# The last pair's round of a stick-breaking attention kernel: VectorE in another order, and eight lower parts of the output weights on GpSimd

## The chip, the cores and the metric

The kernel runs on one core of a Trainium2 chip. What counts is the device time of one execution in microseconds. Five engines run side by side, each through its own list of instructions, and meet at semaphores: TensorE (PE) multiplies, VectorE (DVE) and ScalarE (ACT) work element by element and may read the accumulators (PSUM), GpSimd (POOL) works on the on-chip memory SBUF alone, and SyncE (SP) issues the transfers. Transfers are carried by 16 DMA engines.

## The reference

With one layer only the stick-breaking attention is computed: norm, one input projection to q, k, v and gate, 16 heads of 64, a gated output projection, a residual and a final norm.

```python
h = rmsnorm(x, norm_g[0])                       # x: 1 x 1024 x 1024, float32
q, k, v, gate = jnp.split(h @ w_in, 4, axis=-1)
z = jnp.einsum('bhqd,bhkd->bhqk', q, k) * scale
log_beta = jax.nn.log_sigmoid(z)
log_1m = jnp.where(mask, log_beta - z, 0.0)     # mask: key before query
after = lax.cumsum(log_1m, axis=3, reverse=True) - log_1m
a = jnp.where(mask, jnp.exp(log_beta + after), 0.0)
o = jnp.einsum('bhqk,bhkd->bhqd', a, v)
y = (o * jax.nn.silu(gate)) @ w_out
out = rmsnorm(x + y, final_g)
```

## The kernel before

Products that need float32 are made of three (or two) matmuls of rounded numbers: each operand is split into a high part, a rounded copy, and a **lower part**, the rest after subtraction. A lower part is one `tensor_tensor` with `subtract`, and the high part comes before it, mostly from ScalarE.

The heads are worked on in eight pairs. A round of a pair has 16 **slots**; slot s makes the scores of one head (s // 8) and one block of 128 queries (s % 8), so that the width grows from 128 to 1024 keys in slots 0 to 7 and again in 8 to 15. In every slot the chain is: TensorE makes z (L581); ScalarE makes two sigmoids of it, `rest` (L809) and beta in `a_group` (L811); VectorE turns `rest` into a product along the keys by a scan (L1016); GpSimd multiplies the two (L1115, `a_ready`); TensorE transposes the blocks of the result into `t_ps` (L644); ScalarE copies them to `aT` or `aT_pad` (L794) and VectorE makes the lower part (L1000, `t_lo`); TensorE multiplies with v into `o_ps` (L632). Transposes of a slot take a group of four query blocks that was finished four slots before: those of slot 8 need `a_ready` of slot 7. When a group is done, ScalarE shifts (L786) and VectorE adds (L990) it into `oT`; in slots 1 and 5 GpSimd multiplies `oT` by the gate (L1103), and in slots 2 and 6 ScalarE and VectorE split it (L800, L1006) for SyncE to store.

Between these steps TensorE has other work that fills it up. In the last pair's round it is the gate's projection in slots 0 to 7 (L486) and, from slot 8 on, early blocks of the output projection (L561), listed by slot in `EARLY_BY_SLOT`: two in each of slots 8, 9 and 10, one in slot 11. In a slot they come before the products with v. An early block b of the first output tile needs the stored output of pair b back in `hT` (`o_loaded`, L427) and the output weight block b in its two parts (`wo_ready` at least b + 1).

A gate half is evacuated in slots 0, 4 and 8: ScalarE copies it to `stage` and takes its sigmoid, and VectorE multiplies the two (L982, `gate_ready`).

The **output weight blocks** 0 to 7 come in the last pair's round too. `wo_raw` is a ring of four; SyncE loads blocks 0 to 3 early, and block n from 4 on when `wo_ready` has reached n - 3 (L420). ScalarE makes the high part of the blocks listed for the slot in `WO_BY_SLOT` (`wo_hi`), and VectorE, behind its scan of the same slot, the lower part (`wo_lo_part`, L314, `wo_ready`):

```python
WO_BY_SLOT = {5: (0,), 6: (1,), 7: (2,), 8: (3,), 9: (4, 5), 10: (6,), 12: (7,)}
```

The loads of SyncE stand in one written order: load 4, outputs of pair 2, load 5, output 3, two stores (L395), load 6, outputs 4 and 5, load 7, output 6, two blocks of x, and then the other halves of the outputs. Each output is two loads, of its high and its lower part.

The order on each engine is that of the program: the functions `slot(p, par, s)` of the engines, called by `over_pairs`. `is_last(p)` is true in the round of the last pair, number 7.

Of the kernel before, what the change touches and what calls it, by code (L numbers as in the profile page):

```python
# [29 lines left out]
HALF = 512  # L30
# [96 lines left out]
def evac_at(p, s):  # L127

    if s % 2 or is_tail(p) or (is_first(p) and s == 0):
        return None  # L130
    number = 2 * UNITS0 + 8 * p + s // 2 - 1
    if s == 0:
        return "g", 1, number
    if is_last(p):
        return ("g", s // 4 - 1, 2 * UNITS0 + 8 * p + s // 4 - 1) if s in (4, 8) else None
    return kind_of(p, s - 1), ((s - 1) % 4) // 2, number


def gate_at(p, s):

    evac = evac_at(p, s)
    if not evac or evac[0] != "g":
        return None
    return evac[1], 2 * p - 1 if s == 0 else 2 * p + evac[1]
# [33 lines left out]
def stick_breaking_layer(nc, x, norm_g, w_in, w_out, final_g, out):  # L178
# [3 lines left out]
    with ExitStack() as ctx:  # L182
# [666 lines left out]
        def _(dve):  # L849
# [80 lines left out]
            def heads_lo(kind, par, half, buf, count):  # L930

                dve.wait_ge(qk_hi, count)
                cols = slice(half * HALF, (half + 1) * HALF)
                for hh in range(2):
                    rows = slice(HD * hh, HD * hh + HD)
                    other = slice(HD - HD * hh, 2 * HD - HD * hh)
                    to = q_of(par, hh) if kind == "q" else k_of(par, hh, False)
                    last = nc.vector.tensor_tensor(to[other, cols], stage[rows, buf, :],  # L938
                                                   to[rows, cols].bitcast(F32), ALU.subtract)
                last.then_inc(qk_split, 1)  # L940
# [27 lines left out]
                wait_wo(dve, n)  # L968
                nc.vector.tensor_copy(w_out_of(n // KB, 0)[:, n % KB, :], wo_raw[:, n % WO_RING, :]).then_inc(wo_hi, 1)

            def slot(p, par, s):
                evac = evac_at(p, s)
                if evac:
                    kind, half, h = evac
                    if kind in "kq":
                        heads_lo(kind, 1 - par, half, half, 4 * p + 5 + half + (2 if kind == "q" else 0))
                if gate_at(p, s):

                    half, number = gate_at(p, s)
                    dve.wait_ge(gate_sig, number + 1)  # L980
                    cols = slice(half * HALF, (half + 1) * HALF)
                    nc.vector.tensor_tensor(gate[:, cols], stage[:, half, :], gate[:, cols], ALU.mult  # L982
                                            ).then_inc(gate_ready, 1)
                if s % 4 == 1 and av_at(p, s - 1) and (not is_tail(p) or s < 9):
                    _, _, ohh, grp, _ = av_at(p, s - 1)[-1]
                    group = {1: -1, 5: 0, 9: 1, 13: 2}[s]
                    dve.wait_ge(o_shift, 4 * p + group)
                    rows = slice(HD * ohh, HD * ohh + HD)
                    cols = slice(grp * HALF, (grp + 1) * HALF)
                    nc.vector.tensor_tensor(oT[rows, cols], o_ps[rows, :], oT[rows, cols], ALU.add  # L990
                                            ).then_inc(o_summed, 1)

                for t, av, _, grp, j in (units_at(p, s - 1) if s else av_at(p, 0)):
                    rel = max(0, j - GQ * grp)
                    dve.wait_ge(t_hi, t_base(p) + t + 1)
                    if rel == GQ - 1:
                        hi, lo = aT_pad[:, 0, P:2 * P], aT_pad[:, 1, P:2 * P]
                    else:
                        hi, lo = aT[:, av % 2, 0, rel * P:HALF], aT[:, av % 2, 1, rel * P:HALF]
                    nc.vector.tensor_tensor(lo, t_ps[t % 2][:, rel * P:HALF], hi.bitcast(F32), ALU.subtract  # L1000
                                            ).then_inc(t_lo, 1)
                if s in (2, 6) and not is_first(p):
                    half = s // 4
                    dve.wait_ge(o_hi, 2 * p - 1 + half)
                    hi, lo = split_of(p, half)
                    nc.vector.tensor_tensor(lo, oT[:, half * HALF:(half + 1) * HALF], hi.bitcast(F32),  # L1006
                                            ALU.subtract).then_inc(o_lo, 1)
                if is_tail(p):
                    return

                width = P * (s % 8 + 1)
                span = rest[:, s % 2, S - 1:(S - 1 - width if width < S else None):-1]
                if is_first(p) and s == 0:
                    dve.wait_ge(restart_ready, 1)
                dve.wait_ge(rest_ready, SLOTS * p + s + 1)
                nc.vector.tensor_tensor_scan(span, span, restart[:, S - 1:(S - 1 - width if width < S else None):-1],  # L1016
                                             0.0, ALU.mult, ALU.max).then_inc(scan_done, 1)
                if v_t_at(p, s) is not None:
                    t = v_t_at(p, s)
                    v_lo(1 - par, s // 8, t_base(p) + t, t % 2)  # L1020
                if is_last(p):
                    for n in WO_BY_SLOT.get(s, ()):
                        dve.wait_ge(wo_hi, n + 1)
                        wo_lo_part(nc.vector, n)
                if is_last(p) and s in PARTIAL_SLOTS:

                    n = PARTIAL_SLOTS.index(s)
                    dve.wait_ge(partial_done, n + 1)
                    dve.wait_ge(xs_loaded[n], 16)
                    nc.vector.tensor_tensor(stage[:, n, :], proj_ps[:, :], stage[:, n, :], ALU.add  # L1030
                                            ).then_inc(partial_sum, 1)
# [44 lines left out]
        @block.gpsimd  # L1076
        def _(pool):
            pool.dma_start(g_col[:, :], norm_g).then_inc(g_loaded, 16)

            nc.gpsimd.memset(ident[:, :], 0.0).then_inc(zeros_ready, 1)  # L1080
            pool.wait_ge(zeros_ready, 1)
            nc.gpsimd.affine_select(out=ident[:, :], in_=ident[:, :], compare_op=ALU.not_equal, fill=1.0, base=0,
                                    pattern=[[-1, P]], channel_multiplier=1).then_inc(consts_ready, 1)
            nc.gpsimd.memset(restart[:, 0:S - P], 0)
            pool.wait_ge(consts_ready, 2)
            nc.gpsimd.tensor_copy(restart[:, S - P:S], ident[:, :]).then_inc(restart_ready, 1)

            def lo_w(n, ring, part):
                pool.wait_ge(w_hi, n + 1)
                to = w_split[:, ring, :, 4 * part:4 * part + 4, :]  # L1090
                nc.gpsimd.tensor_tensor(to[:, 1], w_raw[:, part, :].rearrange("p (b n) -> p b n", b=4),  # L1091
                                        to[:, 0].bitcast(F32), ALU.subtract).then_inc(w_ready, 1)

            for n in range(2 * UNITS0 + 2):
                lo_w(n, (n // 2) % 2, n % 2)

            def slot(p, par, s):
                if s in (1, 5) and not is_first(p):
                    half = s // 4
                    pool.wait_ge(o_summed, 4 * p - 1 + half)  # L1100
                    pool.wait_ge(gate_ready, 2 * p - 1 + half)
                    cols = slice(half * HALF, (half + 1) * HALF)
                    nc.gpsimd.tensor_tensor(oT[:, cols], oT[:, cols], gate[:, cols], ALU.mult  # L1103
                                            ).then_inc(o_gated, 1)
                if is_tail(p):
                    return

                i = s % 8
                width = P * (i + 1)
                a = a_g[i // GQ][:, i % GQ, 0:width]  # L1110
                if is_first(p) and s == 0:
                    pool.wait_ge(consts_ready, 2)
                pool.wait_ge(beta_ready, SLOTS * p + s + 1)
                pool.wait_ge(scan_done, SLOTS * p + s + 1)
                nc.gpsimd.tensor_tensor(a, a, rest[:, s % 2, S + 1 - width:S + 1], ALU.mult  # L1115
                                        ).then_inc(a_ready, 1)
                if s % 2 and not is_last(p):
                    part = s % 4 // 2
                    lo_w(2 * (UNITS0 + 4 * p + s // 4 + 1) + part, (UNITS0 + 1 + s // 4) % 2, part)

            over_pairs(pool, slot)


            for n in range(KB, 2 * KB):
                pool.wait_ge(wo_hi, n + 1)
                wo_lo_part(nc.gpsimd, n)
# [24 lines left out]
```

## Time and profile before

| | us |
|---|---|
| median of 3 runs | 697.34 |
| lowest and highest of them | 697.03, 698.51 |
| the profiled execution, its own time | 696.88 |
| its span, first to last instruction | 694.8 |
| busy in the span: TensorE | 670.2 (96%) |
| VectorE | 481.4 (69%) |
| ScalarE | 426.4 (61%) |
| GpSimd | 282.0 (41%) |

The profile gives every instruction's start and length from the span's start. An instruction's length begins when its waits on semaphores are over, so that what it waits for behind that, a port for instance, is in its length. The last pair's round runs from about 546 to 610 us, its slots 5 to 10 from about 564 to 590. "Idle before" is the time for which the engine had nothing running, with the engine, tile and line that ended it. TensorE's weight loads run beside its matmuls.

### The profile page before, as it was taken

The numbers are of one execution on the slowest core, as the hardware profiler recorded it, in microseconds if no ns is written. First come the engines' busy times: TensorE is split into PE (matmuls) and PEld (weight loads), VectorE is DVE, ScalarE is ACT, GpSimd is POOL, SyncE is SP. The second block draws the span as 40 slices with busy tenths as digits, with TensorE's granted clock in tenths as the row PEclk, the third lists the DMA queues.
The fourth block names the chain that finished last, engine by engine and source line by source line (L and its number), as shares of the span: only waits on it lengthen the run. The fifth ranks groups of instructions, "written<-read, shape, count | busy, mean of one in ns | idle before, by whom it ended". The sixth has DMA issues, their size and how long they took to land.

```text
span 694.8 us, 10872 instructions
## 1 busy us (share of the span) xinstructions
PE 670.2 (96%) x3426; PEld 563.4 (81%) x3426; DVE 481.4 (69%) x636; ACT 426.4 (61%) x795; POOL 282.0 (41%) x225
## 2 busy tenths in 40 slices
PE   5999999999999999999999999999999997999995
PEld 4787888888888888888888888888888776888884
DVE  5835666776678677867776677667766798735565
ACT  5614767676767676767676767666766675622333
POOL 2122434453545445444554454435353543315100
PEclk9999999999999999999999999999999999999999
DMA  7131301241114110410042014201420148523332
GB/s 288 46 95 43 92 31 31 61 122 33 31 51 131 31 33 33 136 44 20 25 129 67 16 32 121 76 15 30 121 60 30 61 137 290 211 92 94 125 145 92
DMA packets 28122, 57.64 MB, mean 83 GB/s; under 512 B 3376, under 2 KB 3376, under 8 KB 28080
## 3 DMA queue, kind: packets, MB, share of 16 engines
q1 hardware_dynamic: 25312, 51.13, 24.0%
q10 hardware_dynamic: 2736, 6.03, 2.3%
q8 instruction: 16, 0.26, 0.2%
q14 instruction: 26, 0.21, 0.1%
q0 software_dynamic: 32, 0.00, 0.0%
HBM read 37.23 MB, written 11.53 MB: 70 GB/s over the span
## 4 chain that ended last, share of the span: by engine, by line
PE 90%; DVE 5%; ACT 2%; DMA 1%; POOL 1%; issue 1%; ACTq 0%; DVEq 0%; POOLq 0%
PE proj_ps L486 46%; PE o_ps L632 10%; PE z_ps L581 9%; PE t_ps L644 9%; PE z_ps L561 8%; PE proj_ps L561 4%; PE o_ps L486 2%; DVE rest L1016 2%; PE t_ps L495 1%; DMA a_group<-x 1%; DVE gate L982 1%; ACT stage L719 1%; PE z_ps L506 1%; DVE arena L314 0%; DVE aT L1000 0%
## 5 line engine op out<-in xcount | busy, mean ns | idle before, releaser
L486 PE MATMUL proj_ps<-hT,w_split 128*128 128x512 f32 x1464 | 359.9, 394 | 2.2 <-DVE hT L889 1.4
L486 PEld LDWEIGHTS proj_ps<-hT,w_split 128*128 128x128 f32 x1464 | 270.0, 188 | 57.6 <-DVE hT L889 2.3
L1115 POOL TENSOR_TENSOR a_group<-a_group,rest 128x128 f32<-128x128 f32 (+7 forms) x128 | 158.0, 1235 | 300.0 <-DVE rest L1016 300.0
L1016 DVE TENSOR_TENSOR_SCAN rest<-rest,restart 128x128 f32<-128x128 f32 (+7 forms) x128 | 203.6, 1591 | 16.0 <-ACT rest L809 15.5
L1000 DVE TENSOR_TENSOR aT<-t_ps,aT 128x512 fp32r<-128x512 f32 (+2 forms) x160 | 93.1, 607 | 35.1 <-ACT aT L794 33.6
L794 ACT ACTIVATE aT<-t_ps 128x512 fp32r<-128x512 f32 (+2 forms) x160 | 80.2, 532 | 59.2 <-PE t_ps L644 57.6
L1091 POOL TENSOR_TENSOR w_split<-w_raw,w_split 128x512 fp32r<-128x512 f32 x64 | 91.7, 1434 | 38.1 <-DVE w_split L851 38.1
L581 PE MATMUL z_ps<-arena 128*128 128x512 f32 (+2 forms) x384 | 96.3, 366 | 0.3 <-DVE arena L938 0.3
L938 DVE TENSOR_TENSOR arena<-stage,arena 64x512 fp32r<-64x512 f32 x64 | 44.0, 687 | 67.9 <-ACT arena L739 67.3
L809 ACT ACTIVATE rest<-z_ps 128x128 f32<-128x128 f32 (+7 forms) x128 | 83.9, 655 | 8.9 <-PE z_ps L581 8.6
L644 PE MATMUL t_ps<-ident,a_group 128*128 128x128 f32 x576 | 84.6, 274 | 0.4 <-POOL a_group L1115 0.4
L811 ACT ACTIVATE a_group<-z_ps 128x128 f32<-128x128 f32 (+7 forms) x128 | 84.4, 659 | 0.0
L632 PE MATMUL o_ps<-aT,arena 128*128 128x512 f32 (+2 forms) x320 | 82.7, 364 | 1.7 <-DVE aT L1000 1.7
L644 PEld LDWEIGHTS t_ps<-ident,a_group 128*128 128x128 f32 x576 | 70.0, 142 | 8.5 <-issue 0.6
L719 ACT ACTIVATE stage<-proj_ps 128x512 f32<-128x512 f32 x61 | 36.5, 598 | 61.3 <-PE proj_ps L486 61.3
L632 PEld LDWEIGHTS o_ps<-aT,arena 128*128 128x128 f32 x320 | 59.5, 188 | 16.6 <-DVE aT L1000 4.2
L581 PEld LDWEIGHTS z_ps<-arena 128*128 128x128 f32 x384 | 59.6, 190 | 5.2 <-DVE arena L938 0.8
L561 PE MATMUL z_ps<-arena,hT 128*128 128x512 f32 x246 | 57.7, 391 | 0.0
L786 ACT ACTIVATE oT<-o_ps 64x512 f32<-64x512 f32 x32 | 19.0, 593 | 62.2 <-PE o_ps L632 62.2
L561 PEld LDWEIGHTS z_ps<-arena,hT 128*128 128x128 f32 x246 | 45.8, 188 | 9.4
L990 DVE TENSOR_TENSOR oT<-o_ps,oT 64x512 f32<-64x512 f32 x32 | 22.0, 689 | 25.6 <-ACT oT L786 25.3
L746 ACT ACTIVATE w_split<-w_raw 128x512 fp32r<-128x512 f32 x56 | 35.9, 641 | 0.6
(86 smaller groups left out, 460.7 us busy)
## 6 DMA issues: line engine op xcount, KB each, us to landing
w_raw<-w_in SPq DMA_DIRECT2D x64, 256.0 KB, 2.6
arena<-arena SPq DMA_DIRECT2D x32, 256.0 KB, 4.3
wo_raw<-w_out SPq DMA_DIRECT2D x16, 256.0 KB, 3.8
o_hi_scratch<-o_split SPq DMA_DIRECT2D x14, 256.0 KB, 2.1
o_lo_scratch<-o_split SPq DMA_DIRECT2D x14, 256.0 KB, 2.4
hT<-o_hi_scratch SPq DMA_DIRECT2D x14, 256.0 KB, 4.9
hT<-o_lo_scratch SPq DMA_DIRECT2D x14, 256.0 KB, 6.0
a_group<-x SPq DMA_DIRECT2D x14, 256.0 KB, 3.6
```

The lines of the kernel that those rows point to most:

```text
L486: mm = nc.tensor.matmul(bank[:, :], w_split[:, ring, wl, b, :], hT[:, hl, b, half * HALF:(half + 1) * HALF], start=(b == 0 and n == 0), st ...
L561: mm = nc.tensor.matmul(bank[:, :], hT[:, ol, b, tokens], w_out_of(nh, wl)[:, b, :], start=(b == first and m == 0), stop=(b == last and m ...
L581: mm = nc.tensor.matmul(z[:, c0:c1], q, k_of(par, hh, swapped)[:, c0 - first:c1 - first], start=not swapped, stop=swapped)
L632: mm = nc.tensor.matmul(o_ps[:, c:HALF], v_of(apar)[:, j, 2 * ahh:2 * ahh + 2, :] .rearrange("p x d -> p (x d)"), moving, start=(j == 0 an ...
L644: last = nc.tensor.transpose(t_ps[t % 2][:, i2 * P:(i2 + 1) * P], a_g[grp][:, i2, j * P:(j + 1) * P], ident[:, :])
L794: nc.scalar.activation(to, t_ps[t % 2][:, rel * P:HALF], ACT.Copy).then_inc(t_hi, 1)
L809: nc.scalar.activation(rest[:, s % 2, S - width:S], z_ps[s % 2][:, first:first + width], ACT.Sigmoid, scale=-SCALE).then_inc(rest_ready, 1)
L811: nc.scalar.activation(a_g[grp][:, i % GQ, 0:width], z_ps[s % 2][:, first:first + width], ACT.Sigmoid, scale=SCALE).then_inc(beta_ready, 1)
L1000: nc.vector.tensor_tensor(lo, t_ps[t % 2][:, rel * P:HALF], hi.bitcast(F32), ALU.subtract).then_inc(t_lo, 1)
L1016: nc.vector.tensor_tensor_scan(span, span, restart[:, S - 1:(S - 1 - width if width < S else None):-1], 0.0, ALU.mult, ALU.max).then_inc(s ...
L1091: nc.gpsimd.tensor_tensor(to[:, 1], w_raw[:, part, :].rearrange("p (b n) -> p b n", b=4), to[:, 0].bitcast(F32), ALU.subtract).then_inc(w_ ...
L1115: nc.gpsimd.tensor_tensor(a, a, rest[:, s % 2, S + 1 - width:S + 1], ALU.mult).then_inc(a_ready, 1)
```

## The change

In the last pair's round VectorE does the sum of a finished group and the lower parts of `aT` (now the function `heads_out`) before the gate product; in the other rounds the order is as it was. And in that round the lower parts of blocks 0 to 7 of the output weights are made by GpSimd, in the same slots, each behind GpSimd's own product of the slot.

```diff
-            def slot(p, par, s):
-                evac = evac_at(p, s)
...
+            def heads_out(p, s):
+
                 if s % 4 == 1 and av_at(p, s - 1) and (not is_tail(p) or s < 9):
...
+            def slot(p, par, s):
+                if is_last(p):
+                    heads_out(p, s)
+                evac = evac_at(p, s)
...
+                if not is_last(p):
+                    heads_out(p, s)
                 if s in (2, 6) and not is_first(p):
...
-                if is_last(p):
-                    for n in WO_BY_SLOT.get(s, ()):
-                        dve.wait_ge(wo_hi, n + 1)
-                        wo_lo_part(nc.vector, n)
                 if is_last(p) and s in PARTIAL_SLOTS:
...
                 nc.gpsimd.tensor_tensor(a, a, rest[:, s % 2, S + 1 - width:S + 1], ALU.mult
                                         ).then_inc(a_ready, 1)
+                if is_last(p):
+                    for n in WO_BY_SLOT.get(s, ()):
+                        pool.wait_ge(wo_hi, n + 1)
+                        wo_lo_part(nc.gpsimd, n)
                 if s % 2 and not is_last(p):
```

VectorE, slots 5 to 8 of the last pair's round, before. A row is the line, the operation, what is written and read, and the shape; the scan is called SCALAR_TENSOR_TENSOR here:

```order
L1016 SCALAR_TENSOR_TENSOR rest<-rest,restart 128x768
L314 TENSOR_TENSOR arena<-wo_raw,arena 128x512
L1000 TENSOR_TENSOR aT<-t_ps,aT 128x384
L1006 TENSOR_TENSOR o_split<-oT,o_split 128x512
L1016 SCALAR_TENSOR_TENSOR rest<-rest,restart 128x896
L314 TENSOR_TENSOR arena<-wo_raw,arena 128x512
L1000 TENSOR_TENSOR aT<-t_ps,aT 128x256
L1016 SCALAR_TENSOR_TENSOR rest<-rest,restart 128x1024
L314 TENSOR_TENSOR arena<-wo_raw,arena 128x512
L982 TENSOR_TENSOR gate<-stage,gate 128x512
L1000 TENSOR_TENSOR aT_pad<-t_ps,aT_pad 128x128
L1016 SCALAR_TENSOR_TENSOR rest<-rest,restart 128x128
```

The same place in the changed kernel, whose lines have other numbers (the scan is L1023, the lower parts of aT L989, the gate product L1005, the split L1013):

```order
L1023 SCALAR_TENSOR_TENSOR rest<-rest,restart 128x768
L989 TENSOR_TENSOR aT<-t_ps,aT 128x384
L1013 TENSOR_TENSOR o_split<-oT,o_split 128x512
L1023 SCALAR_TENSOR_TENSOR rest<-rest,restart 128x896
L989 TENSOR_TENSOR aT<-t_ps,aT 128x256
L1023 SCALAR_TENSOR_TENSOR rest<-rest,restart 128x1024
L989 TENSOR_TENSOR aT_pad<-t_ps,aT_pad 128x128
L1005 TENSOR_TENSOR gate<-stage,gate 128x512
L1023 SCALAR_TENSOR_TENSOR rest<-rest,restart 128x128
```

The three L314 are gone from VectorE, and the gate product stands behind the lower part of the padded tile.

GpSimd, slots 5 to 9 of the same round, before:

```order
L1103 TENSOR_TENSOR oT<-oT,gate 128x512
L1115 TENSOR_TENSOR a_group<-a_group,rest 128x768
L1115 TENSOR_TENSOR a_group<-a_group,rest 128x896
L1115 TENSOR_TENSOR a_group<-a_group,rest 128x1024
L1115 TENSOR_TENSOR a_group<-a_group,rest 128x128
L1115 TENSOR_TENSOR a_group<-a_group,rest 128x256
```

and in the changed kernel, where the product of a slot is L1118 and the gating product L1106:

```order
L1106 TENSOR_TENSOR oT<-oT,gate 128x512
L1118 TENSOR_TENSOR a_group<-a_group,rest 128x768
L314 TENSOR_TENSOR arena<-wo_raw,arena 128x512
L1118 TENSOR_TENSOR a_group<-a_group,rest 128x896
L314 TENSOR_TENSOR arena<-wo_raw,arena 128x512
L1118 TENSOR_TENSOR a_group<-a_group,rest 128x1024
L314 TENSOR_TENSOR arena<-wo_raw,arena 128x512
L1118 TENSOR_TENSOR a_group<-a_group,rest 128x128
L314 TENSOR_TENSOR arena<-wo_raw,arena 128x512
L1118 TENSOR_TENSOR a_group<-a_group,rest 128x256
L314 TENSOR_TENSOR arena<-wo_raw,arena 128x512 x2
```

The parts of blocks 0 to 5 now stand between GpSimd's products. TensorE's, ScalarE's and SyncE's orders are the same in both kernels.

## Rows read from the trace of the kernel before

**Rows 1.** Timeline of TensorE, 545 to 611 us: start, length, operation [idle before]

```profile
549.45 0.50 PE L632 MATMUL o_ps<-aT_pad,arena 128*128 128x256 f32 x2 [1.15 <-DVE aT_pad L1000]
...
552.11 1.33 PE L632 MATMUL o_ps<-aT,arena 128*128 128x512 f32 x4
...
573.68 0.51 PE L632 MATMUL o_ps<-aT,arena 128*128 128x256 f32 x2 [1.18 <-DVE aT L1000]
...
574.61 1.55 PE L561 MATMUL proj_ps<-arena,hT 128*128 128x512 f32 x6
580.32 0.79 PE L632 MATMUL o_ps<-aT_pad,arena 128*128 128x256 f32 x2 [4.16 <-DVE aT_pad L1000]
580.91 1.91 PE L644 MATMUL t_ps<-ident,a_group 128*128 128x128 f32 x8
...
586.44 1.54 PE L561 MATMUL proj_ps<-arena,hT 128*128 128x512 f32 x6
...
592.95 3.02 PE L561 MATMUL proj_ps<-arena,hT 128*128 128x512 f32 x12 [0.18 <-DVE stage L1030]
...
610.60 1.06 PE L644 MATMUL t_ps<-ident,a_group 128*128 128x128 f32 x8 [0.39 <-POOL a_group L1115]
```

**Rows 2.** Busy times in windows: five engines, then the clock's share, DMA's, GB/s

```profile
579.00:580.00 1.00, 0.00 (x0) 0.00 (x0) 1.00 (x2) 0.00 (x0) 0.52 (x1) 0.92 0.93 287
...
583.00:584.00 1.00, 1.00 (x5) 0.81 (x4) 0.84 (x2) 1.00 (x4) 0.00 (x0) 0.87 1.09 350
```

**Rows 3.** Timeline of VectorE, 545 to 606 us

```profile
547.24 1.95 DVE L982 TENSOR_TENSOR gate<-stage,gate 128x512 f32<-128x512 f32 x1 [0.75 <-ACT gate L776]
...
549.32 1.29 DVE L1016 TENSOR_TENSOR_SCAN rest<-rest,restart 128x128 f32<-128x128 f32 x1
...
560.97 1.17 DVE L982 TENSOR_TENSOR gate<-stage,gate 128x512 f32<-128x512 f32 x1 [0.62 <-ACT gate L776]
...
565.44 1.75 DVE L1016 TENSOR_TENSOR_SCAN rest<-rest,restart 128x768 f32<-128x768 f32 x1
567.10 1.72 DVE L314 TENSOR_TENSOR arena<-wo_raw,arena 128x512 fp32r<-128x512 f32 x1
...
570.70 2.01 DVE L1016 TENSOR_TENSOR_SCAN rest<-rest,restart 128x896 f32<-128x896 f32 x1
572.64 0.66 DVE L314 TENSOR_TENSOR arena<-wo_raw,arena 128x512 fp32r<-128x512 f32 x1
...
573.55 3.53 DVE L1016 TENSOR_TENSOR_SCAN rest<-rest,restart 128x1024 f32<-128x1024 f32 x1
577.00 0.66 DVE L314 TENSOR_TENSOR arena<-wo_raw,arena 128x512 fp32r<-128x512 f32 x1
577.59 2.48 DVE L982 TENSOR_TENSOR gate<-stage,gate 128x512 f32<-128x512 f32 x1
```

**Rows 4.** Timeline of GpSimd, 545 to 606 us

```profile
565.49 2.79 POOL L1103 TENSOR_TENSOR oT<-oT,gate 128x512 f32<-128x512 f32 x1
568.24 1.99 POOL L1115 TENSOR_TENSOR a_group<-a_group,rest 128x768 f32<-128x768 f32 x1
572.86 2.08 POOL L1115 TENSOR_TENSOR a_group<-a_group,rest 128x896 f32<-128x896 f32 x1 [2.63 <-DVE rest L1016]
577.23 2.29 POOL L1115 TENSOR_TENSOR a_group<-a_group,rest 128x1024 f32<-128x1024 f32 x1 [2.29 <-DVE rest L1016]
```

**Rows 5.** Instructions on wo_raw: ns min/median/max, first and last start

```profile
L314 POOL TENSOR_TENSOR arena<-wo_raw,arena x8: 1294/1298/1490, 632.3 to 643.9; 128x512 fp32r<-128x512 f32 x8
```

**Rows 6.** Timeline of SyncE's issues, 540 to 640 us

```profile
577.69 0.34 SPq L420 DMA_DIRECT2D wo_raw<-w_out  x1
...
579.50 0.43 SPq L427 DMA_DIRECT2D hT<-o_lo_scratch  x1
```

**Rows 7.** us from issue to landing: the issue of 579.50, then the page's median

```profile
hT<-o_lo_scratch SPq DMA_DIRECT2D x1, 256.0 KB, 5.2
...
hT<-o_lo_scratch SPq DMA_DIRECT2D x14, 256.0 KB, 6.0
```

More of the change, by code:

```diff
@@ L969, in wo_hi_part @@
                 nc.vector.tensor_copy(w_out_of(n // KB, 0)[:, n % KB, :], wo_raw[:, n % WO_RING, :]).then_inc(wo_hi, 1)
-            def slot(p, par, s):
-                evac = evac_at(p, s)
[L973 to L983, printed above, removed]
+            def heads_out(p, s):
                 if s % 4 == 1 and av_at(p, s - 1) and (not is_tail(p) or s < 9):
@@ L1001, in slot @@
                                             ).then_inc(t_lo, 1)
+            def slot(p, par, s):
+                if is_last(p):
+                    heads_out(p, s)
+                evac = evac_at(p, s)
+                if evac:
+                    kind, half, h = evac
+                    if kind in "kq":
+                        heads_lo(kind, 1 - par, half, half, 4 * p + 5 + half + (2 if kind == "q" else 0))
+                if gate_at(p, s):
+                    half, number = gate_at(p, s)
+                    dve.wait_ge(gate_sig, number + 1)
+                    cols = slice(half * HALF, (half + 1) * HALF)
+                    nc.vector.tensor_tensor(gate[:, cols], stage[:, half, :], gate[:, cols], ALU.mult
+                                            ).then_inc(gate_ready, 1)
+                if not is_last(p):
+                    heads_out(p, s)
                 if s in (2, 6) and not is_first(p):
```

## The prediction

> **What bounds the kernel now.** I read the chain of waits first, then the timelines of the four engines over the last pair's round, and last SyncE's queue. TensorE is busy nearly everywhere, so a change in this round is worth what it does to TensorE's gaps there, and to waits that are hidden today. The largest gaps are 1.15 us in slot 0, 1.18 us in slot 7, and 4.16 us in slot 8, which ends at 580.32 [rows 1]. The last one costs more than its length: 3.7 us after TensorE stopped (576.16) the granted clock fell from its 2.4 GHz level to the 1.2 GHz one, from 579.84 to 583.26, as the shares 0.92 and 0.87 of two windows give [rows 2]. In it eight transposes took 1.91 us, and 1.06 elsewhere [rows 1].
>
> The gap of slot 8 ends with VectorE's lower part of the padded tile. Ahead of it VectorE ran without a pause: scans, lower parts of aT, three lower parts of output weight blocks (L314) and the gate product [rows 3]. Several took far longer than their work. The gate product took 2.48 us and ended 0.55 us after GpSimd's product of 577.23 (2.29 us, to 579.52); the scan of 1024 took 3.53 us and ended 2.14 us after GpSimd's product of 572.86 (to 574.94); the first L314 took 1.72 us and the second 0.66 [rows 3, 4]. The other way round, GpSimd's gating product dispatched at 565.49 took 2.79 us, and ended 1.09 us after VectorE's scan of 565.44 (to 567.19) [rows 3, 4]. So instructions of VectorE with two SBUF inputs and GpSimd's products take turns, the one dispatched first going first. I call that the port. This is what the sum is made with.
>
> **Part 1, the other order.** It acts in slots 0, 4 and 8. In slot 0 the gate product (547.24, 1.95 us) holds up the lower part, and TensorE loses 1.15 us [rows 1, 3]. With the order changed this gap goes, but the gate product still ends behind GpSimd at 549.19, the next scan still ends at 550.61 behind GpSimd's weight part, and o_sum and two lower parts follow as now, for which TensorE's o_ps of 552.11 waits at the end of slot 1 [rows 1, 3]. Gained: 0 to 0.1 us; I take 0. In slot 4 the gate product (1.17 us from 560.97) stands before lower parts that TensorE hardly waits for, and the scan behind both moves by under 0.1 us: 0. In slot 8 it takes the lower part out from behind 2.48 us. That gain depends on part 2.
>
> **Part 2, the eight lower parts on GpSimd.** Each leaves VectorE (0.66 us free of a wait, [rows 3]) and costs 1.30 us on GpSimd [rows 5], 1.10 when it has waited for the port (the 1.09 above, same shape). Each still needs the port, twice as long as before. In slots 5 to 8 the port has no room. I walk it from 567.19, where the scan of slot 5 ends in both kernels:
> gating product to 568.28 as now; product of slot 5 to 569.8 (1.4 us behind the port now, about 1.5 here; now 570.23 as L314 is ahead); o_split's lower part, 0.55, to 570.35; block 0's part, queued on GpSimd since 569.8 and so ahead of the scan, 1.1, to 571.45; scan of 896, 1.86 behind the port (2.01 free), to 573.3, now 572.71; product of slot 6, 0.15 to start and 1.8, to 575.25; scan of 1024, 2.14, to 577.4, now 577.08; block 1's part 1.1, to 578.5; gate product 0.55, to 579.05; product of slot 7, 1.86 (what 577.23 took once the port was free at 577.66), to 580.9, now 579.52; scan of 128, 0.3, to 581.2; block 2's part to 582.3; product of slot 8, 0.4, to 582.7; block 3's part, 1.3, to 584.0 [rows 3, 4, 5]. ScalarE's copies of the blocks, for which the parts wait too, were there for VectorE's parts of 572.64 and 577.00 [rows 3] and don't hold them.
>
> What TensorE sees of it. The lower part of slot 8 is ready at 577.7 instead of just before 580.32. But three other things come late. First, the second early block of slot 8 needs wo_ready 2, that is block 1's part, at 578.5; today it is hidden. TensorE does it then and goes on with o_ps to about 579.7. Second, the transposes of slot 8 need a_ready of slot 7 at 580.9; they start at 580.91 now [rows 1]. So of the 4.16 us nothing comes back there. Third, in slot 9 the early blocks 2 and 3 need the parts that end at 582.3 and 584.0: blocks done by 584.7, o_ps then, about 0.3 us later than now. The 0.85 us of slow transposes are saved and waited away again here.
>
> **Part 3, SyncE's queue, which is the term that decides.** A raw block is reloaded when a part has been made: load 6 waits for wo_ready 3. Now that is VectorE's L314 of 577.00, done at 577.66, and the load goes out at 577.69; behind it stand the four loads of stored outputs 4 and 5, the last at 579.50 [rows 3, 6]. With block 2's part at 582.3 load 6 goes at 582.33 and the last of the four 1.81 us later, at 584.15. It lands 5.2 us after issue now [rows 7]: 589.35. TensorE wants it in slot 10, in the second of the two early blocks that start at 586.44 and end at 587.98 now [rows 1]. It is hidden by over 3 us today; then it is not: 589.35 and three matmuls of 0.23 give 590.05, 2.07 us later. Output 6, behind load 7, goes at about 585.4, lands by 591 and is wanted at 592.0, and the parts 4 to 6 are done by 586.4, 587.6 and 591.2, each before its use: hidden, by 0.8 us at the least.
>
> After slot 10 VectorE has pauses, and TensorE's gaps are 0.18 us at 592.95 and 0.39 at 610.60 [rows 1]; both end chains that TensorE's own work starts, so they move along. Blocks 6 and 7 on GpSimd free 1.3 us of VectorE where nobody waits for it: 0. The sum is +2.05 us, from 0 (part 1), 0 (slot 8), and +2.05 (slot 10, which contains the +0.3 of slot 9). On the profiled execution's own 696.88 that is 698.9; on the median of 697.34 it is 699.4.
>
> The Trainium skill (Perfetto Trace Analysis, Optimizing Scalar/DVE Operations) says of moving work between VectorE and GpSimd that, since they share a port, it "might not help". By that the sum would be 0; this trace agrees that they take turns (the 2.48 us product, [rows 3]).
>
> **Rivals.** (a) *The gain arrives*: GpSimd's extra parts hide beside VectorE's scans, without turns. Then, from 567.19, the scan of 1024 ends about 576.0, the product of slot 7 about 578.0, transposes 2.9 us earlier; but block 2's part ends about 579.3, 1.6 us after 577.66, so the load lands about 586.3 and slot 10's blocks end about 587.0: 1.0 us gained, 696.3. It needs the port to be free for these parts, against all four stretched rows; were the loads of no account it would be up to 3 us. 0.15. (b) *The loads are hidden after all*, because they land faster from a queue that stood empty: then part 5 of GpSimd, done at 587.6, decides, +0.3, 697.6; between this and the forecast lies up to +1.3. 0.20. (c) *Worse*: the page's median from issue to landing is 6.0 us and not 5.2 [rows 7], +0.8; and TensorE's pieces of idling (3.1, 1.2, 0.8, 0.8 us) bring the clock down again, about +0.9 as the slow transposes show: +3.8, 701.1. For the clock speaks the fall at 579.84, against it that no single gap reaches the 3.7 us before that fall. 0.10. (d) That the change doesn't do what it says: the rows of the order show both parts of it, so this gets no chance of its own. The forecast keeps 0.55, between +1.4 and +3.2.
>
> **The numbers.** 0.2% is 1.4 us, about what a measurement of this kernel can tell from no change. Slower by more: forecast and (c), 0.65. Within: (b) and half of (a), 0.27. Faster by more: the rest of (a), 0.08. The range leaves out that rest and the upper part of (c): 696.5 to 701.2.
>
> **What would show it.** Lower parts of L314 on GpSimd of 1.3 us or more, block 1's ending near 578.5 and block 2's near 582.3; TensorE's gap before slot 8's padded o_ps short, but transposes of slot 8 still near 581; two waits in slots 8 and 9 at L561 for GpSimd's L314, and one in slot 10 for a landing of stored output; slot 10's early blocks ending near 590. Load 6 issued before 580, or transposes of slot 8 before 579.5, would prove the walk wrong; slot 10 without a wait for a landing would leave me with (b).

## The result

The changed kernel takes 700.47 us in the median of 6 runs (699.96 to 701.58); the kernel before took 697.13 beside it (6 runs). The ratio is 1.0044, with a 95% interval of 1.0034 to 1.0054: slower by 3.1 us by the ratio, and by 3.3 us between the two medians. Forecast was +2.05 us, or 699.4 us, in a range from 696.5 to 701.2.

The profiled execution took 701.32 us, its span is 699.5 (before: 696.88 and 694.8). That pair differs by 4.4 us, more than the medians. Of that, 0.81 us come from TensorE's first projection of the last pair's round, which starts at 547.50 and not at 546.69, as it did before. They lie ahead of everything that was changed; that start was anywhere from 546.5 to 547.5 in the profiles of this study. To compare a time of after with one of before, take 0.81 off.

### The profile after

The timeline of TensorE, columns as in rows 1 (start, length, operation, idle before it and what ended it):

```profile
549.59 1.06 PE L644 MATMUL t_ps<-ident,a_group 128*128 128x128 f32 x8 [0.22 <-POOL a_group L1118]
...
552.92 1.33 PE L632 MATMUL o_ps<-aT,arena 128*128 128x512 f32 x4 [0.87 <-DVE aT L989]
...
575.28 0.87 PE L561 MATMUL proj_ps<-arena,hT 128*128 128x512 f32 x3
579.16 1.10 PE L561 MATMUL proj_ps<-arena,hT 128*128 128x512 f32 x3 [3.01 <-POOL arena L314]
...
581.65 1.94 PE L644 MATMUL t_ps<-ident,a_group 128*128 128x128 f32 x8 [0.97 <-POOL a_group L1118]
583.25 2.92 PE L561 MATMUL proj_ps<-arena,hT 128*128 128x512 f32 x6
...
590.50 0.93 PE L561 MATMUL proj_ps<-arena,hT 128*128 128x512 f32 x3 [1.91 <-DMA hT<-o_lo_scratch]
591.81 0.93 PE L561 MATMUL proj_ps<-arena,hT 128*128 128x512 f32 x3 [0.37 <-DMA hT<-o_lo_scratch]
```

These rows answer rows 1. The gap of 1.15 us in slot 0 is gone, and in its place stand 0.22 us for GpSimd's product and 0.87 us one slot later: the o_ps of 552.92 is that of 552.11 before, less 0.81 to the hundredth. In slot 8 the padded product no longer waits 4.16 us for VectorE. The second early block waits 3.01 us for GpSimd's lower part of block 1 instead, and the transposes wait for GpSimd's product. Then in slot 10 both early blocks wait for the landing of a stored output, and the second of them ends at 592.74, which is 591.93 on the clock of before: 3.95 us behind 587.98.

VectorE and GpSimd, slots 6 to 9:

```profile
570.87 3.11 DVE L1023 TENSOR_TENSOR_SCAN rest<-rest,restart 128x896 f32<-128x896 f32 x1
...
574.22 3.82 DVE L1023 TENSOR_TENSOR_SCAN rest<-rest,restart 128x1024 f32<-128x1024 f32 x1
...
578.15 1.50 DVE L1005 TENSOR_TENSOR gate<-stage,gate 128x512 f32<-128x512 f32 x1
579.57 2.21 DVE L1023 TENSOR_TENSOR_SCAN rest<-rest,restart 128x128 f32<-128x128 f32 x1
```

```profile
570.36 1.74 POOL L314 TENSOR_TENSOR arena<-wo_raw,arena 128x512 fp32r<-128x512 f32 x1
574.13 1.77 POOL L1118 TENSOR_TENSOR a_group<-a_group,rest 128x896 f32<-128x896 f32 x1 [2.02 <-DVE rest L1023]
575.86 3.25 POOL L314 TENSOR_TENSOR arena<-wo_raw,arena 128x512 fp32r<-128x512 f32 x1
579.07 2.44 POOL L1118 TENSOR_TENSOR a_group<-a_group,rest 128x1024 f32<-128x1024 f32 x1
581.47 1.39 POOL L314 TENSOR_TENSOR arena<-wo_raw,arena 128x512 fp32r<-128x512 f32 x1
...
583.19 1.28 POOL L314 TENSOR_TENSOR arena<-wo_raw,arena 128x512 fp32r<-128x512 f32 x1
```

Every one of the walk's turns can be read off here. The scan of 896, 2.01 us before [rows 3], is 3.11 long, because block 0's part went first and ended at 572.10. The scan of 1024 waits for the product that ends at 575.90; block 1's part, dispatched at 575.86, waits for the scan (578.04) and ends at 579.11; the gate product follows, to 579.65, the product of slot 7 to 581.51, the scan of 128, and block 2's part to 582.86.

SyncE's issues, and below them the time from issue to landing of the transfer of 584.71:

```profile
579.13 0.33 SPq L420 DMA_DIRECT2D wo_raw<-w_out  x1
...
580.92 0.43 SPq L395 DMA_DIRECT2D o_lo_scratch<-o_split  x1
582.88 0.34 SPq L420 DMA_DIRECT2D wo_raw<-w_out  x1
583.26 0.45 SPq L427 DMA_DIRECT2D hT<-o_hi_scratch  x1
583.76 0.43 SPq L427 DMA_DIRECT2D hT<-o_lo_scratch  x1
584.23 0.43 SPq L427 DMA_DIRECT2D hT<-o_hi_scratch  x1
584.71 0.43 SPq L427 DMA_DIRECT2D hT<-o_lo_scratch  x1
```

```profile
hT<-o_lo_scratch SPq DMA_DIRECT2D x1, 256.0 KB, 7.0
```

Load 5 goes out 0.02 us after block 1's part (579.13, behind 579.11), and load 6 (582.88) 0.02 us after block 2's part; before, load 6 went at 577.69 [rows 6]. The transfer that slot 10 waits for lands 7.0 us after its issue, against 5.2 before [rows 7]. The chain that ended last takes just this way (start, length, what):

```profile
579.07 2.44 POOL a_group L1118
581.51 1.36 POOL arena L314
582.86 0.02 issue
582.88 0.34 SPq L420
...
584.71 6.96 DMA hT<-o_lo_scratch
591.67 0.14 issue
591.81 0.93 PE proj_ps L561 x3
```

From block 2's part to the end of the second early block of slot 10, a step of it for each engine that the forecast named.

### The profile page after: what moved, and what is told of

Read it like the earlier page. It is cut to its first block, busy times and chain, and to the rows that moved or that the text cites. A ratio compares the mean times of both kernels' runs of the same rounds, so it can differ in the third digit from the quotient of the medians.

```text
span 699.5 us, 10872 instructions
## 1 busy us (share of the span) xinstructions
PE 672.8 (96%) x3426; PEld 565.7 (81%) x3426; DVE 475.7 (68%) x628; ACT 426.4 (61%) x795; POOL 292.2 (42%) x233
## 4 chain that ended last, share of the span: by engine, by line
PE 89%; DVE 4%; POOL 2%; DMA 2%; ACT 1%; issue 1%; SPq 0%; ACTq 0%; POOLq 0%; DVEq 0%
PE proj_ps L486 46%; PE o_ps L632 10%; PE z_ps L581 9%; PE t_ps L644 8%; PE z_ps L561 8%; PE proj_ps L561 4%; PE o_ps L486 2%; DVE rest L1023 1%; PE t_ps L495 1%; POOL a_group L1118 1%; DMA hT<-o_lo_scratch 1%; PE z_ps L514 1%; DMA a_group<-x 1%; DVE hT L889 1%; PE z_ps L506 1%
## 5 line engine op out<-in xcount | busy, mean ns | idle before, releaser
L1118 POOL TENSOR_TENSOR a_group<-a_group,rest 128x128 f32<-128x128 f32 (+7 forms) x128 | 156.0, 1219 | 295.3 <-DVE rest L1023 295.3
L1023 DVE TENSOR_TENSOR_SCAN rest<-rest,restart 128x128 f32<-128x128 f32 (+7 forms) x128 | 206.9, 1617 | 16.1 <-ACT rest L809 15.5
L989 DVE TENSOR_TENSOR aT<-t_ps,aT 128x512 fp32r<-128x512 f32 (+2 forms) x160 | 93.1, 607 | 43.3 <-ACT aT L794 41.7
L561 PE MATMUL proj_ps<-arena,hT 128*128 128x512 f32 x138 | 35.9, 406 | 5.5 <-POOL arena L314 3.0
```

Of the source, the lines that this page charges most:

```text
L561: mm = nc.tensor.matmul(bank[:, :], hT[:, ol, b, tokens], w_out_of(nh, wl)[:, b, :], start=(b == first and m == 0), stop=(b == last and m ...
```

## The experiments

Each row is one kernel. All ratios are to the kernel before in the same comparison. Its median was 697.13 us beside the changed kernel and 697.6 to 698.0 beside the others, so compare two rows by their ratios.

| kernel | us, median | ratio, 95% interval |
|---|---|---|
| the changed kernel | 700.47 | 1.0044, 1.0034 to 1.0054 |
| order alone | 696.20 | 0.9974, 0.9964 to 0.9984 |
| order in slot 8 alone | 696.35 | 0.9975, 0.9962 to 0.9988 |
| lower parts alone | 700.98 | 1.0044, 1.0031 to 1.0058 |
| blocks 1 and 2 alone on GpSimd | 700.07 | 1.0035, 1.0023 to 1.0047 |
| blocks 4 to 7 alone on GpSimd | 696.60 | 0.9985, 0.9976 to 0.9994 |
| changed, loads apart | 698.03 | 1.0005, 0.9996 to 1.0014 |
| changed, stores first | 699.68 | 1.0025, 1.0016 to 1.0034 |
| late parts (meant faster) | 696.61 | 0.9985, 0.9976 to 0.9994 |
| changed, fills for parts | 697.99 | one run |
| changed, pause behind output 5 | 702.10 | one run |

### The two parts of the change, each alone

The order alone: VectorE keeps the eight lower parts (the edit against the changed kernel, shortened).

```diff
+                if is_last(p):                      # VectorE, behind its scan
+                    for n in WO_BY_SLOT.get(s, ()):
+                        dve.wait_ge(wo_hi, n + 1)
+                        wo_lo_part(nc.vector, n)
...
-                if is_last(p):                      # GpSimd
-                    for n in WO_BY_SLOT.get(s, ()):
-                        pool.wait_ge(wo_hi, n + 1)
-                        wo_lo_part(nc.gpsimd, n)
```

> Part 1 alone: VectorE's other order in the last pair's round, the eight lower parts on VectorE as before. Theory (the lower parts on GpSimd cost the time, the order alone frees TensorE in slot 8): the gate product no longer stands before the padded lower part, the product of slot 7 on GpSimd ends near 579.5 as before, the transposes of slot 8 start there instead of 580.9, the clock doesn't fall, and slot 9's o_ps comes about 2 us earlier: 694.9 to 696.0 us. Rival (TensorE waits for something else at the same time, the scan of 128 or the parts of blocks 2 and 3): no change, 697.1.

Measured: 696.20 us, ratio 0.9974: the kernel before is beaten by 1.8 us. That is 0.2 us above the range that was expected. TensorE's timeline of slots 8 and 9, and VectorE's:

```profile
577.76 0.50 PE L632 MATMUL o_ps<-aT_pad,arena 128*128 128x256 f32 x2 [1.76 <-DVE aT_pad L989]
579.51 1.06 PE L644 MATMUL t_ps<-ident,a_group 128*128 128x128 f32 x8 [1.25 <-POOL a_group L1123]
580.33 1.63 PE L561 MATMUL proj_ps<-arena,hT 128*128 128x512 f32 x6
```

```profile
577.43 0.28 DVE L989 TENSOR_TENSOR aT_pad<-t_ps,aT_pad 128x128 fp32r<-128x128 f32 x1
577.63 2.28 DVE L1005 TENSOR_TENSOR gate<-stage,gate 128x512 f32<-128x512 f32 x1
```

The gate product is as long as before (2.28 us, behind GpSimd), but nobody waits for it. The gap of 4.16 us has become 1.76 and 1.25. The eight transposes take 1.06 us and not 1.91, since the clock did not fall in this execution. It is the fastest of the nine (694.78 us), and the theory's "the clock doesn't fall" held in it and, by the mean clock of 0.998, in one other; the last section shows what that is worth. The rival is out.

The lower parts alone: `heads_out` is called behind the gate product in every round.

> Part 2 alone: the eight lower parts on GpSimd, VectorE's order as before. Theory (the queue of loads behind wo_ready decides, whatever VectorE's order): as the changed kernel, 700.0 to 701.0 us. Rival (the two parts of the change work against each other, since the later gate product puts GpSimd's product of slot 7 off): better than the changed kernel by the 0.55 us that the gate product holds the port, 699.6 or less.

Measured: 700.98 us, ratio 1.0044, the changed kernel's own. Block 1's part and the product of slot 7 are 3.25 and 2.44 us long, as in the changed kernel, and slot 10 waits for the landings:

```profile
590.12 0.93 PE L561 MATMUL proj_ps<-arena,hT 128*128 128x512 f32 x3 [2.60 <-DMA hT<-o_lo_scratch]
591.45 0.94 PE L561 MATMUL proj_ps<-arena,hT 128*128 128x512 f32 x3 [0.40 <-DMA hT<-o_lo_scratch]
```

So on top of the lower parts on GpSimd the order is worth nothing that was measured: its gain is real only while something else isn't later.

The order in slot 8 alone (in slots 0 and 4 the gate product first, as before; all parts on VectorE):

> VectorE's other order in slot 8 alone; in slots 0 and 4 the gate product first as before, all lower parts on VectorE. Theory (the order is worth nothing in slots 0 and 4, because TensorE waits for the same scan and lower parts one slot later): as the order in all three slots, 695.7 to 696.7 us. Rival (the gap of 1.15 us in slot 0 counts): 1 us more, 697.0 or over.

Measured: 696.35 us, ratio 0.9975. Its slot 0 has the gap of 1.15 us again, and no cost of it shows: the ratio is that of the order alone (0.9974), within the intervals.

### Which of the eight parts

Blocks 0 to 3 back on VectorE, in the slots and places of before, 4 to 7 on GpSimd; the order as in the change:

> VectorE's other order, the lower parts of blocks 0 to 3 back on VectorE, those of 4 to 7 on GpSimd. Theory (only wo_ready 2 to 4 on GpSimd does harm, in slots 6 to 8): the loads go out as early as before, the parts of blocks 4 and 5 are late for slot 10 by about 1 us at the most: 695.2 to 697.0 us. Rival (GpSimd is too slow for any of them): 698 or more.

Measured: 696.60 us, ratio 0.9985. In slot 10 TensorE waits for the parts of blocks 4 and 5, by 0.66 and 0.28 us. That is the late part of 1 us that was expected, no more.

Blocks 1 and 2 on GpSimd and the other six on VectorE, with waits on `wo_ready` that keep the eight in order:

> VectorE's other order, only the lower parts of blocks 1 and 2 on GpSimd, the other six on VectorE (with waits that keep wo_ready in order). Theory (the delay of load 6 behind the part of block 2 is what costs): these two carry nearly all of it, since block 1 stands before GpSimd's product of slot 7 and block 2 releases load 6: 699.3 to 700.5 us. Rival (the cost is spread over the eight by their time on GpSimd): a quarter of the way from 696.2 to 700.5, 697.3.

Measured: 700.07 us, ratio 1.0035. Two parts out of eight carry nearly all of the loss. The part of block 1 alone is 3.25 us long here too:

```profile
574.95 3.25 POOL L314 TENSOR_TENSOR arena<-wo_raw,arena 128x512 fp32r<-128x512 f32 x1
```

SyncE's load 6 goes out at 581.97 instead of 577.69; 0.56 us of these 4.28 lie ahead of the round (547.25 against 546.69).

### The loads

The changed kernel, with the stored outputs taken out from behind the raw blocks:

```diff
             load_wo(4)
             load_o(0, 2)
-            load_wo(5)
             load_o(0, 3)
             slot(PAIRS - 1, 1, 7)
-            load_wo(6)
             load_o(0, 4)
             load_o(0, 5)
-            load_wo(7)
+            load_wo(5)
+            load_wo(6)
             sp.wait_ge(o_stored, 64 * (PAIRS - 1))
             load_o(0, PAIRS - 2)
+            load_wo(7)
```

> The changed kernel with the stored outputs 3 to 6 taken out from behind the raw weight blocks 5 to 7 in SyncE's list, so that their loads don't wait for wo_ready. Theory (the landing of stored outputs in slot 10 decides): the two waits for it in slot 10 go, the part of block 5 on GpSimd is next to be late, and 2.5 to 3.3 us come back: 697.2 to 698.2 us. Rival (the lower parts themselves, by the turns at the port, cost the time): 0 to 1 us comes back, 699.5 to 700.5.

Measured: 698.03 us, ratio 1.0005. All of the loss against the kernel before is gone but a few tenths, with every lower part still on GpSimd and every turn at the port as it was (block 1's part 3.25 us, the product of slot 7 2.44 us):

```profile
578.61 0.96 PE L561 MATMUL proj_ps<-arena,hT 128*128 128x512 f32 x3 [3.01 <-POOL arena L314]
...
581.11 1.94 PE L644 MATMUL t_ps<-ident,a_group 128*128 128x128 f32 x8 [1.30 <-POOL a_group L1118]
...
588.26 1.55 PE L561 MATMUL proj_ps<-arena,hT 128*128 128x512 f32 x6
```

TensorE's waits of slot 8 are those of the changed kernel, 3.01 us and more. Slot 10's six matmuls go without a wait. So the turns at the port are the cause of the delay, and SyncE's order turns it into the loss against the kernel before. The turns have a price of their own too: this kernel is 1.8 us slower than the order alone (698.03 and 696.20, in one comparison), and in the profiles two things are later in it. Its transposes of slot 8 wait for GpSimd until 581.11 and not until 579.51. And the part that is next to be late was not block 5's, as expected, but block 6's: in slot 11 TensorE waits 0.77 us for it. What each is worth was not run apart. What the loads apart would do to the kernel before, on their own, was not run.

Why the landing was 1.8 us later than forecast was tried twice. First the stores of slot 7 moved ahead of load 5:

```diff
             load_wo(4)
             load_o(0, 2)
+            slot(PAIRS - 1, 1, 7)
             load_wo(5)
             load_o(0, 3)
-            slot(PAIRS - 1, 1, 7)
             load_wo(6)
```

> The changed kernel with SyncE's two stores of slot 7 moved ahead of load 5, so that they go out near 573.5 and not in the pack of ten transfers that begins with load 5 near 579. The issues of the stored outputs 4 and 5 stay where they are, since they wait for wo_ready 3. Theory (the landing was 1.8 us later than forecast because ten transfers of 256 KB stand in one pack): eight are left, the last landing of slot 10 comes about 1.2 us earlier, 699.0 to 699.8 us. Rival (the time from issue to landing there has another cause than what was issued before it): no change, 700.4 to 701.

Measured: 699.68 us, ratio 1.0025. Output 5 lands 6.0 us after its issue:

```profile
hT<-o_lo_scratch SPq DMA_DIRECT2D x1, 256.0 KB, 6.0
```

That is 1.0 us sooner, with two transfers of 256 KB fewer ahead of it, where 1.2 were expected. The profiled execution took 701.30 us all the same, and is the slowest of its kernel's eleven: in it the clock fell a second time, near 590.5, and the three groups of matmuls from there took 1.31, 1.91 and 1.40 us, against 0.93, 1.10 and 0.93 in the changed kernel's profile. Then a pause behind it, so that nothing follows until it has landed (`sp.wait_ge(o_loaded[0][5], 32)` ahead of `load_wo(7)`):

> The changed kernel with a pause in SyncE's list: load 7 and all behind it go out only when stored output 5 has landed. For the trace alone; output 6 comes later and the time is longer for it. Theory (the landing of output 5, 6.96 us after its issue in the changed kernel and 5.2 before, shares the 16 DMA engines with what is issued right behind it; before there was a pause of 1.3 us there): it lands 5.0 to 5.7 us after its issue. Rival (only what was issued ahead of it counts, the pack since load 5): 6.6 us or more, as in the changed kernel.

Measured: 6.8 us from issue to landing. My theory of that run fell, and the rival's 6.6 or more came: what is issued behind the transfer gives 0.2 us here.

What is still under way ahead of it counts. SyncE's issues alone don't show it: the ten transfers from load 5 to output 5 go out from 579.13 to 584.71 with a pause of 1.5 us ahead of load 6, and before they went from 573.32 to 579.50 with one of 2.1 us. But the second store, of 580.92, lands 5.2 us after its issue, and so it is still under way when output 5 is issued; before, that of 575.12 took 4.4 us and landed at 579.50, just as output 5 went out. Counting by the traces the transfers of SyncE that were issued and hadn't landed when output 5 was issued:

| kernel | under way | issue to landing of output 5, us |
|---|---|---|
| before | 4, a fifth landing just then | 5.2 |
| changed, stores first | 4 | 6.0 |
| changed, fills for parts (next section) | 4 | 6.0 |
| lower parts alone | 5 | 6.7 |
| changed, pause behind output 5 | 5 | 6.8 |
| blocks 1 and 2 alone on GpSimd | 5 | 7.0 |
| the changed kernel | 6 | 7.0 |

The stores explain 1.0 of the 1.8 us as measured. The other 0.8 stay open: with four under way, as before, two kernels still needed 6.0 us. Only the kernel before had four ahead and also 1.3 us without an issue behind, and that pair was not run apart.

### The port

GpSimd's lower parts are replaced by fills, which write the same tile and read nothing. The lower parts of the first half of w_out are left out of the computation:

```diff
-                        wo_lo_part(nc.gpsimd, n)
+                        nc.gpsimd.memset(w_out_of(0, 1)[:, n, :].bitcast(F32), 0.0).then_inc(wo_ready, 1)
```

> The changed kernel with GpSimd's eight lower parts made fills with zero, which write SBUF and read nothing; the lower parts of w_out's first half are left out of the computation. Theory (VectorE's instructions and GpSimd's take turns where both read SBUF through one port): the scan of 896, 3.11 us in the changed kernel, is back to 2.0, and a fill dispatched while a scan runs doesn't wait for it; the scan of 1024 is still stretched by GpSimd's product before it, to about 3.5. Slot 8's transposes come near 579.5. Rival (any work of GpSimd holds VectorE up): the scan of 896 stays above 2.5 us by the length of the fill, and fills dispatched in a scan are stretched.

VectorE's scans and GpSimd's instructions beside them:

```profile
569.87 2.01 DVE L1023 TENSOR_TENSOR_SCAN rest<-rest,restart 128x896 f32<-128x896 f32 x1
...
572.12 3.83 DVE L1023 TENSOR_TENSOR_SCAN rest<-rest,restart 128x1024 f32<-128x1024 f32 x1
```

```profile
569.35 0.52 POOL L1123 MEMSET arena<- 128x512 f32 x1
572.03 1.78 POOL L1118 TENSOR_TENSOR a_group<-a_group,rest 128x896 f32<-128x896 f32 x1 [2.17 <-DVE rest L1023]
573.75 0.53 POOL L1123 MEMSET arena<- 128x512 f32 x1
```

The scan of 896 is back to 2.01 us. That alone proves little, as the fill of 569.35 had ended (569.87) when the scan was dispatched. The fill of 573.75 is the test. It was dispatched as the scan of 1024 got its turn (573.81, where the product ended), and took 0.53 us beside it, like the one that had no scan beside it (0.52). The scan wasn't held up either: it ended at 575.95, 2.14 us after the product, as it did before behind its product [rows 3, 4]. It is still stretched by the product before it. So, as far as this one overlap shows, it isn't GpSimd's being busy that makes the two take turns, but its reading. The Trainium skill (SBUF — State Buffer, Who interferes with whom) states this: a VectorE instruction with two SBUF inputs contends with a GpSimd instruction that reads SBUF, not with one that only writes. This trace agrees: 0.53 us for the fill beside a scan, where block 1's part, which reads, took 3.25. The transposes of slot 8 start at 578.74, sooner than the expected 579.5, and slot 10 still waits for landings (1.49 and 1.30 us), since load 6 waits behind the fill that follows the product of slot 7.

### A version meant to be faster

The order alone, with the parts of blocks 0, 1 and 2 each moved behind `heads_out` of the next slot, and the loads apart:

> A version meant to be faster: VectorE's other order with all lower parts on VectorE (as in the run of the order alone), those of blocks 0, 1, 2 each moved behind the lower parts of aT of the next slot, and SyncE's loads apart from wo_ready. Theory (the transposes of slot 8 wait for GpSimd's product of slot 7, and that for the part of block 2 that took the port just before it): the product ends 0.4 us earlier, the small gaps of slots 6 and 7 shrink without effect on the end: 0.3 to 0.8 us under the order alone, 695.4 to 695.9 us. Rival (the parts are late for the early blocks of slot 8): no better than the order alone, 696.2 or more.

Measured: 696.61 us, ratio 0.9985, not under the order alone. This was a miss, and the trace shows the turn that I had the wrong way round:

```profile
573.44 2.22 DVE L314 TENSOR_TENSOR arena<-wo_raw,arena 128x512 fp32r<-128x512 f32 x1
575.59 2.28 DVE L1026 TENSOR_TENSOR_SCAN rest<-rest,restart 128x1024 f32<-128x1024 f32 x1
577.79 0.26 DVE L989 TENSOR_TENSOR aT_pad<-t_ps,aT_pad 128x128 fp32r<-128x128 f32 x1
577.97 0.68 DVE L314 TENSOR_TENSOR arena<-wo_raw,arena 128x512 fp32r<-128x512 f32 x1
```

```profile
578.01 2.49 POOL L1126 TENSOR_TENSOR a_group<-a_group,rest 128x1024 f32<-128x1024 f32 x1 [2.89 <-DVE rest L1026]
```

Block 2's part stands behind the padded lower part now, which takes no turn and only 0.2 us. It was still dispatched 0.04 us before GpSimd's product (577.97 and 578.01), and so the product waits for it as before. Block 1's part stands right before the scan of 1024 and waits 1.6 us of its 2.22 for GpSimd. The product ends at 580.50, 0.5 us later than in the order alone when the starts of the two profiles (547.38 and 546.71) are set off. The fastest version stays the order alone, in slot 8 or in all three slots.

## Why the prediction was right, point by point

**The port and its turns: right, to 0.35 us in every step.** Less the 0.81 us, the ends measured are: block 0's part 571.29 (forecast 571.45), scan of 896 573.17 (573.3), product of slot 6 575.09 (575.25), scan of 1024 577.23 (577.4), block 1's part 578.30 (578.5), gate product 578.84 (579.05), product of slot 7 580.70 (580.9), scan of 128 580.97 (581.2), block 2's part 582.05 (582.3), block 3's part 583.66 (584.0).

**Part 1 worth nothing here: right**, in slot 0 by the trace of after and by the run of slot 8 alone, in slot 8 by the run of the parts alone. The forecast said that its gain in slot 8 depends on part 2, but not what it is worth without part 2: 1.8 us, by the run of the order alone.

**SyncE's queue decides: right**, shown by the loads taken apart (2.7 us come back, from the ratios 1.0044 and 1.0005 of some 698 us). Load 6 went at 582.07 on the clock of before (forecast 582.33), the last of the four at 583.90 (584.15).

**The term that was mis-sized is the landing**: 7.0 us and not 5.2. The mechanism was right, and this size in it was not. With 7.0 the profiles' own sum closes: +2.05, +1.76 for the landing (6.96 less 5.2), +0.38 for the 0.14 us behind it and the 0.93 of the three matmuls taken at 0.69, and -0.25 for the earlier issue, make +3.94, where 3.95 was measured at the end of slot 10. Behind it nothing is lost or gained: the gap at 592.95 of before [rows 1] is there again, 0.18 us at 597.69, 4.74 us later, as the spans are 4.7 apart. I had taken the landing of a transfer of before, which had four others under way ahead of it, for one that the change itself gives six; that is 1.0 of the 1.8 us, and for 0.8 the cause stays open. The page's median of 6.0 [rows 7] stood in a rival and would have been nearer. The same term was short for output 6, which the forecast called hidden by 0.8 us at the least: it too takes 7.0 us and lands 1.9 us later than forecast. It stays hidden, by 1.0 us, only because slot 10 is later than forecast too.

That the median still came within 1.1 us of the forecast (700.47 and 699.4), with a landing 1.8 us off, is in part luck. The pair of profiles, less the 0.81 us, is 3.9 us apart in its spans and 3.6 in its times, but the medians only 3.3, and nothing in the forecast made that difference. A loss of 3.1 to 3.3 us lies at the upper end of the +1.4 to +3.2 that the forecast kept for itself, and the end of the range, 701.2, is there for rival (c).

**Rival (c) had both of its mechanisms, and neither of its prices.** The landing came later by 1.8 us and not by 0.8. The clock fell too, near 579.8, and stayed at 1.2 GHz to about 586.6 (windows; the clock's share is the third number from the end):

```profile
579.00:580.00 1.00, 0.84 (x3) 0.72 (x4) 1.00 (x2) 0.00 (x0) 1.00 (x2) 0.91 0.00 0
...
586.00:587.00 1.00, 1.00 (x5) 0.82 (x4) 0.00 (x0) 0.00 (x0) 1.00 (x2) 0.68 1.08 186
```

Six matmuls took 2.92 us for it (583.25), and yet it cost nothing in this execution: TensorE then waited 1.91 us for the landing. My argument against the fall, that no single gap reaches 3.7 us, didn't hold: the longest here was 3.01.

**Rival (a), the gain arrives, and (b), the loads hidden, are out**; (b) comes near what the loads taken apart make of the kernel (ratio 1.0005).

## What to carry to other kernels

Before work moves from VectorE to GpSimd, list which instructions of both read SBUF at the place, VectorE's with two inputs, and walk their turns: there 0.66 us that were hidden became 3.25. Then follow every semaphore that the moved instruction releases, into the transfer queue above all: a load waits for its buffer, and what stands behind it in the list waits too, whether it needs the buffer or not. Where a change has two parts, price each alone; here one gained 1.8 us and the other took 4.9 off it, by the ratios 0.9974 and 1.0044. Of these 4.9 us, 2.7 were the queue of transfers; the other 2.2 stay when the loads are taken apart, where GpSimd's product of slot 7 and the part of block 6 are still late. And take the time from issue to landing from a transfer with as many others under way as yours will have.

## What the hardware showed that was not expected

Most of the spread between runs of one kernel goes with the clock. The mean granted clock of each run of the kernel before stands beside its time: those at 0.996 took 696.7 to 697.3 us, those at 0.994 696.7 to 697.5, those at 0.992 took 697.4 to 698.8. Of the order alone, 0.998 (no fall in slots 8 and 9, in the profiled one) goes with 694.8 and 695.3 us, 0.994 to 0.996 with 695.9 to 696.2, and 0.992 with 696.9 to 697.4. The waits are the same in them: the profile of the order alone and that of slot 8 alone have gaps of 1.76 and 1.25, and 1.75 and 1.25 us, at the same place. In the first the clock stays; in the second it falls within the gap (columns as above):

```profile
579.00:580.00 1.00, 0.00 (x0) 0.00 (x0) 1.00 (x1) 0.45 (x1) 0.92 (x1) 0.55 0.78 248
580.00:581.00 1.00, 0.94 (x5) 0.97 (x6) 1.00 (x3) 0.00 (x0) 0.06 (x1) 0.50 0.84 303
```

and the transposes take 1.94 us instead of 1.06. In the changed kernel 0.990 took 699.96 and 700.05 us and 0.994 took 700.07: its landings hide the slow stretch of slots 8 and 9. Its slowest execution, at 0.988, took 701.58; whether the clock fell a second time there, as in the profile with the stores first, no trace shows. A comparison of two kernels near such a gap needs many runs, and one profile of each can differ by over 2 us for this (694.78 and 697.43 us are both of the order alone).
